# Eight key slots and nine value slots for the sample group, value loads issued by ScalarE, and a projection chunk moved between a sample's picks and its values

## The reference, cut to what matters

```python
q, k, v, u, ga, gp = jnp.split(h @ w_in, SPLITS, axis=-1)     # ga, gp: the gates
...
k_past = k_cache[layer, page_table].reshape(b, -1, N_HEADS, 2, HEAD_DIM)
v_past = v_cache[layer, page_table].reshape(b, -1, N_HEADS, V_DIM)
s_past = jnp.einsum('bqhcd,bkhcd->bhcqk', q, k_past)
s_new = jnp.where(tril, jnp.einsum('bqhcd,bkhcd->bhcqk', q, k_new), NEG)
p = softmax(concat(s_past, s_new) * scale); p = p[:, :, 0] - lam * p[:, :, 1]
return einsum('bhqk,bkhe->bqhe', p[..., :n_past], v_past) + einsum(..., p[..., n_past:], v_new)
```

## Time and profile before

| | |
|---|---|
| Time, median of 3 runs | 2114.14 us (2108.64 to 2119.16) |
| Time of the profiled execution | 2115.86 us |
| Its span, first to last instruction | 2114.1 us |
| Mean granted TensorE clock over the span | 0.988 |
| PE busy, share of the span | 2055.5 us, 97% |
| DVE, ACT, POOL busy | 1117.7, 608.3, 496.7 us |
| Head 7 of phase 1 | from 490 to 564 us |
| Phase 2 | from 564 to 858 us |

### The profile page before, as it was taken

One profiled execution on the slowest core, in us unless ns is written; L12 is line 12 of the kernel. 1 busy time (PEld: TensorE's weight loads), 2 busy tenths in 40 slices (PEclk: granted clock), 3 DMA queues, 4 the chain that ended last, 5 costly groups with the idle time before them and its releaser, 6 DMA issues.

```text
span 2114.1 us, 35690 instructions
## 1 busy us (share of the span) xinstructions
PE 2055.5 (97%) x14393; PEld 1863.8 (88%) x14393; DVE 1117.7 (53%) x1471; ACT 608.3 (29%) x1200; POOL 496.7 (23%) x373
## 2 busy tenths in 40 slices
PE   9999999998887989999999999999999999999999
PEld 8888888886775757999999988999999999999997
DVE  6766666664542333266553443554555555555556
ACT  5444445443311111224112422311221122122120
POOL 5333232421111111242331111311221121122120
PEclk9999999999998989999999999999999999999999
DMA  5222212114388786311224320211110111012112
GB/s 150 57 62 57 61 46 56 37 52 122 120 282 286 252 297 210 97 40 50 87 80 124 118 97 11 70 31 41 50 60 12 61 50 41 31 50 61 31 40 96
DMA packets 190791, 189.18 MB, mean 89 GB/s; under 512 B 21536, under 2 KB 164396, under 8 KB 190516
## 3 DMA queue, kind: packets, MB, share of 16 engines
q1 hardware_dynamic: 175660, 176.53, 26.3%
q10 hardware_dynamic: 14992, 10.62, 1.6%
HBM read 162.73 MB, written 24.62 MB: 89 GB/s over the span
## 4 chain that ended last, share of the span: by engine, by line
PE 93%; DMA 3%; SPq 2%; DVE 1%; issue 1%; POOL 0%; ACT 0%; POOLq 0%; DVEq 0%
PE PS L1488 39%; PE PS L2255 13%; PE PS L1016 6%; PE PS L2010 4%; PE PS L282 4%; PE PS L284 4%; PE PS L283 4%; PE PS L338 3%; PE PS L362 3%; DMA v_pg<-in_cache_v_dram 2%; PE PS L1098 2%; PE PS L351 2%; PE PS L1131 1%; PE PS L1509 1%; PE PS L1521 1%
## 5 line engine op out<-in xcount | busy, mean ns | idle before, releaser
L1475 POOL TENSOR_TENSOR fw_lo<-fw_raw,fw_hi 128x1024 fp32r<-128x1024 f32 x86 | 214.6, 2495 | 823.5 <-ACT fw_hi L1471 823.5
L1488 PE MATMUL PS<-m_hi,fw_hi 128*128 128x384 f32 (+1 forms) x1032 | 228.3, 329 | 0.0
L1488 PE MATMUL PS<-m_lo,fw_hi 128*128 128x384 f32 (+1 forms) x1032 | 227.5, 328 | 0.0
L1488 PE MATMUL PS<-m_hi,fw_lo 128*128 128x384 f32 (+1 forms) x1032 | 227.5, 328 | 0.0
L2383 DVE TENSOR_TENSOR x<-x,PS 128x512 f32<-128x512 f32 x198 | 136.2, 688 | 143.6 <-PE PS L2255 143.3
L1488 PEld LDWEIGHTS PS<-m_hi,fw_lo 128*128 128x128 f32 x1032 | 176.3, 188 | 0.0
L1488 PEld LDWEIGHTS PS<-m_lo,fw_hi 128*128 128x128 f32 x1032 | 176.3, 188 | 0.0
L1488 PEld LDWEIGHTS PS<-m_hi,fw_hi 128*128 128x128 f32 x1032 | 176.0, 188 | 0.4 <-POOL fw_lo L1475 0.2
L282 PE MATMUL PS<-w_hi,act_hi 128*128 128x384 f32 (+1 forms) x456 | 164.7, 361 | 0.0
L284 PE MATMUL PS<-w_hi,act_lo 128*128 128x384 f32 (+1 forms) x456 | 153.6, 337 | 0.0
L283 PE MATMUL PS<-w_lo,act_hi 128*128 128x384 f32 (+1 forms) x456 | 153.1, 336 | 0.0
(11 more groups left out here) (316 smaller groups left out, 4235.0 us busy)
## 6 DMA issues: line engine op xcount, KB each, us to landing
k_ring<-in_cache_k_dram SPq DMA_DIRECT2D x64, 512.0 KB, 5.7
v_pg<-in_cache_v_dram SPq DMA_DIRECT2D x56, 512.0 KB, 6.3
fw_raw<-in_w_up_dram SPq DMA_DIRECT2D x44, 512.0 KB, 3.9
fw_raw<-in_w_in_dram SPq DMA_DIRECT2D x24, 512.0 KB, 4.7
wd_raw<-in_w_down_dram SPq DMA_DIRECT2D x22, 512.0 KB, 4.4
w_raw<-in_w_in_dram SPq DMA_DIRECT2D x21, 512.0 KB, 5.2
out_dram<-raw SPq DMA_DIRECT2D x16, 512.0 KB, 3.7
sa_ring<-ga_scratch SPq DMA_DIRECT2D x8, 544.0 KB, 3.6
```

What stands on the lines that cost most here:

```text
L1475: e.tensor_tensor(fw_lo[slot][:, 0:kts, :], fw_raw[:, 0:kts, :], fw_hi[slot][:, 0:kts, :].bitcast(F32), ALU.subtract).then_inc(fw_tail, 1)
L1488: ins = e.matmul(PS[:, 3 * slot + c, 0:cw], w[slot][:, kt, :], x[:, kt, c0:c0 + cw], start=first and kt == 0, stop=last and kt == KT - 1)
```

## The change

The 17 page slots are divided anew: 8 for keys (one sample's), 9 for values; the last sample's values use the value slots too. With 8 slots the key pages of a sample stand in order, and the scores read them as whole rows of 8 pages. SP loads all 8 keys of the next sample in one go when a sample's scores are done. Value loads past the first nine are issued by ACT, after the copy of the third chunk; so are the weight loads of the gate tiles, in `act_chunk`. The stores of a sample's output move from ACT to SP, one sample later. The third chunk moves between the picks and the values, where page 4 used to follow page 3 with the chunk between them. The samples get 6, 5, 4, 4, 4, 4, 3 and 2 chunks instead of 4 each; the first of sample 0's comes before its scores. In head 7 DVE transposes four key pages, at s = 5 to 8, instead of six at s = 1 to 6. SP issues the first four key pages ahead of the head's k and v stores, and two loads of values later; after the head it waits for the last matmul of the head instead of the stores of its output.

```diff
-                if not proj and 1 <= s <= KEYS_TURNED_EARLY:
-                    dve_turn_keys(e, s - 1)
+                if not proj and s > QT - KEYS_TURNED_EARLY:
+                    dve_turn_keys(e, s - QT + KEYS_TURNED_EARLY - 1)
...
-        KEY_GROUP = NPG // 2
-        RK = 3 * KEY_GROUP
+        HALF = NPG // 2
+        RK = NPG
...
+        mid_pg = [r(f"v_pg{j}", [P, NH * VD]) for j in range(2, 6)]
-        KEYS_TURNED_EARLY = KEYS_EARLY // 2 * 2
+        KEYS_TURNED_EARLY = 4
...
-        late_pg = [r(f"v_pg{j}", [P, NH * VD]) for j in range(2, 5)]
+        late_pg = [r(f"v_pg{j}", [P, NH * VD]) for j in range(6, 9)]
...
-        P_PER = (NC * N_FILL - TT - 1) // NB
+        P_EACH = (6, 5, 4, 4, 4, 4, 3, 2)
...
             e.activation(dst, PS[:, PJ + use % 2, 0:cw], ACT.Copy).then_inc(pj_free, 1)
             if c == NC - 1 and n + 2 <= N_U:
                 fm_head(e, n + 2, n % 2)
+            if c == 0 and n >= 1 and n + 2 <= N_U:
+                fm_load(e, n + 2, gate_cols(n + 2) if n + 2 < N_U else w_in_cols(COL_U))
...
-                                           pages[part, :, :, c:c + QB], start=r == 0 and x == 0, stop=r == 1 and x == XB - 1)
+                                           k_ring[part, :, c:c + QB], start=r == 0 and x == 0, stop=r == 1 and x == XB - 1)
...
         def pe_phase2(e):
             pe_chunk(e, P_FIRST, {})
             for b in range(NB):
                 fill = [lambda p=p: pe_chunk(e, p, {}) for p in chunks_of(b)]
+                if b == 0:
+                    fill[0]()
                 pe_scores_of_sample(e, b)
-                fill[0]()
+                if b:
+                    fill[0]()
                 fill[1]()
                 pe_probs(e, b)
-                for j in range(KEY_GROUP):
+                for f in fill[2:3]:
+                    f()
+                for j in range(NPG + 1):
                     pe_value_page(e, b, j)
-                fill[2]()
-                for j in range(KEY_GROUP, NPG + 1):
-                    pe_value_page(e, b, j)
-                fill[3]()
+                for f in fill[3:]:
+                    f()
...
+        def act_load_values(e, b, first, last):
+            for g in range(RV + b * NPG + first, min(RV + b * NPG + last, NB * NPG)):
+                load_values(e, g)
...
                 act_sample_exp(e, b)
-                act_chunk(e, fill[0])
+                if b:
+                    act_chunk(e, fill[0])
                 act_chunk(e, fill[1])
-                if b:
-                    act_stores(e, b - 1)
-                act_chunk(e, fill[2])
+                for p in fill[2:3]:
+                    act_chunk(e, p)
+                act_load_values(e, b, 0, NPG)
                 act_take_values(e, b)
-                act_chunk(e, fill[3])
+                for p in fill[3:]:
+                    act_chunk(e, p)
...
-            e.wait_ge(k_ld[g % RK // 2], 32 * (g // RK + 1))
+            e.wait_ge(k_ld[g % RK // HALF], HALF * 16 * (g // RK + 1))
...
-            for g in range(2):
-                sp_load_values(e, g)
-            sp_store_kv(e, NH - 1, 1)
             e.wait_ge(b7_free, b_use(NH - 2, True, ("o", TT - 1)) + 1)
             e.wait_ge(kv_st[0], NH // 2 * 64 + 1)
-            for g in range(KEYS_EARLY):
+            for g in range(HALF):
+                sp_load_keys(e, g)
+            sp_store_kv(e, NH - 1, 1)
+            for g in range(HALF, KEYS_EARLY):
                 sp_load_keys(e, g)
...
-            for p in range(TT):
-                sp_chunk(e, p)
-            phase1_over(e)
+            for g in range(2):
+                load_values(e, g)
+            e.wait_ge(b7_full, b_use(NH - 1, False, ("o", TT - 1)) + 1)
+            e.wait_ge(kv_st[1], NH // 2 * 64 + 1)
             sp_load_keys(e, KEYS_EARLY)
             for g in range(2, RV):
-                sp_load_values(e, g)
+                load_values(e, g)
...
             for b in range(NB):
                 e.wait_ge(sc_full, b + 1)
-                for g in range(RK + b * NPG, RK + b * NPG + KEY_GROUP):
-                    if g < NB * NPG:
-                        sp_load_keys(e, g)
...
+                for g in range((b + 1) * NPG, min(b + 2, NB) * NPG):
+                    sp_load_keys(e, g)
                 if b + 2 < NB:
                     e.wait_ge(qb_ready, b + 1)
                     sp_load_queries(e, b + 2)
...
+                if b:
+                    store_outputs(e, b - 1)
```

More of the change, by code:

```diff
@@ L957, in build_step @@
         r = Region(RING, R3)
-        v_pg = [r(f"v_pg{j}", [P, NH * VD]) for j in range(2)] + late_pg
+        v_pg = [r(f"v_pg{j}", [P, NH * VD]) for j in range(2)] + mid_pg + late_pg
         RV = len(v_pg)
@@ L962, in build_step @@
         pg_ld = sem("pg_ld")
-        k_ld = [sem(f"k_ld{j}") for j in range(RK // 2)]
+        k_ld = [sem(f"k_ld{j}") for j in range(RK // HALF)]
         v_ld = [sem(f"v_ld{j}") for j in range(RV)]
@@ L988, in build_step @@
         P_FIRST = TT
-        P_PER = (NC * N_FILL - TT - 1) // NB
-        assert TT + 1 + NB * P_PER == NC * N_FILL
+        P_EACH = (6, 5, 4, 4, 4, 4, 3, 2)
+        assert TT + 1 + sum(P_EACH) == NC * N_FILL and len(P_EACH) == NB
         def chunks_of(b):
-            p = P_FIRST + 1 + b * P_PER
-            return range(p, p + P_PER)
+            p = P_FIRST + 1 + sum(P_EACH[:b])
+            return range(p, p + P_EACH[b])
         ga_dram = nc.dram_tensor("ga_scratch", [P, N_SPILLED, TOK], F32, kind="Internal").ap()
@@ L1051, in pool_chunk @@
                 e.wait_ge(fw_tail, n + 3)
[L1053 to L1056, removed]
         def phase1_over(e):
@@ L1064, in phase1_over @@
                 e.wait_ge(kv_st[i], NH // 2 * 64 + 1)
[L1066 to L1074, removed]
         def queries(g, r, x, part):
@@ L1079, in pe_scores_of_sample @@
         def pe_scores_of_sample(e, b):
-            lo, hi, _ = key_groups(b)
-            pages = k_ring[:, :, :].rearrange("p (g j) n -> p g j n", j=KEY_GROUP)[:, lo:hi + 1:hi - lo, :, :]
             e.wait_ge(qb_ready, b + 1)
@@ L1105, in pe_probs @@
             for j in range(NPG):
-                ins = e.matmul(PS[:, B_PTS, j * NH * NS:(j + 1) * NH * NS], es[:, page_block(b, j) * PAGE:][:, 0:PAGE],
+                ins = e.matmul(PS[:, B_PTS, j * NH * NS:(j + 1) * NH * NS], es[:, j * PAGE:(j + 1) * PAGE],
                                pick_r[b % 2][:, :], start=True, stop=True)
@@ L1122, in pe_value_page @@
                 v = v_new
-            elif b == NB - 1:
-                e.wait_ge(k_ld[(END_SLOT + j) // 2], 32 * (NB * NPG // RK + 1))
-                v = k_ring[:, END_SLOT + j, :]
             else:
@@ L1137, in pe_value_page @@
                 ins.then_inc(os_full, 1)
-        END_SLOT = KEY_GROUP
-        assert (NB * NPG - KEY_GROUP) % RK == 0
         def pe_phase2(e):
@@ L1145, in pe_phase2, with store_output @@
                 fill = [lambda p=p: pe_chunk(e, p, {}) for p in chunks_of(b)]
+                if b == 0:
+                    fill[0]()
                 pe_scores_of_sample(e, b)
-                fill[0]()
+                if b:
+                    fill[0]()
                 fill[1]()
                 pe_probs(e, b)
-                for j in range(KEY_GROUP):
+                for f in fill[2:3]:
+                    f()
+                for j in range(NPG + 1):
                     pe_value_page(e, b, j)
-                fill[2]()
-                for j in range(KEY_GROUP, NPG + 1):
-                    pe_value_page(e, b, j)
-                fill[3]()
-        def act_store(e, b, par, h):
+                for f in fill[3:]:
+                    f()
+        def store_output(e, b, par, h):
             e.dma_start(o_dram[bass.ds(SEQ + b * NS, NS), h * VD:(h + 1) * VD],
@@ L1179, in act_phase2, with store_outputs @@
                 fill = chunks_of(b)
+                if b == 0:
+                    act_chunk(e, fill[0])
                 act_sample_exp(e, b)
-                act_chunk(e, fill[0])
+                if b:
+                    act_chunk(e, fill[0])
                 act_chunk(e, fill[1])
-                if b:
-                    act_stores(e, b - 1)
-                act_chunk(e, fill[2])
+                for p in fill[2:3]:
+                    act_chunk(e, p)
+                act_load_values(e, b, 0, NPG)
                 act_take_values(e, b)
-                act_chunk(e, fill[3])
+                for p in fill[3:]:
+                    act_chunk(e, p)
             act_spill(e, NC * N_FILL - 1)
             fm_head(e, N_U + 1, 1)
-            act_stores(e, NB - 1)
-        def act_stores(e, b):
+            store_outputs(e, NB - 1)
+        def store_outputs(e, b):
             e.wait_ge(os_copied, b + 2)
             for h in range(NH):
-                act_store(e, b, b % 2, h)
+                store_output(e, b, b % 2, h)
         def dve_keys(e, step, b):
@@ L1266, in pool_phase2, with load_page @@
                     pool_chunk(e, p)
```

(31 more changed lines are left out.)

## The result

| | Before | After |
|---|---|---|
| Median of the runs | 2113.79 us (2108.64 to 2119.16, 4 runs) | 2095.37 us (2094.09 to 2096.62, 4 runs) |
| Ratio, 95% interval | | 0.9913, 0.9887 to 0.9938 |
| Profiled execution, span | 2115.86, 2114.1 us | 2095.47, 2093.7 us |

The account below looks back on a forecast made before the run. Some 50 us of PE idle, beside time at 1.2 GHz, were all there was to gain. Phase 2 -44.7, head 7 -9.8, scores +5: -49.5 from 2115.9 gives 2066.4; the median lies 1.7 under: 2065 us, range 2048 to 2091.

Parts of the forecast that it names:

- Scores under DMA load: Scores of samples 1 to 7: value pages landing into them cost PE +5 us, bounds 0 and 27.
- sample 0's 3.9: Extra PE loss per sample when scores run under load, 4.3 us in sample 0's against 0.4 each in samples 1 to 7.
- PE starves at every score: Rival, phase 2 scores: the 3.9 us come in full seven times, 2087 us; chance 0.15.
- ACT's wait in head 7: Chunk 3 of head 7: weight loads moved to ACT wait 6.6 us for POOL's split; PE loses 3, bounds 0 and 6.6.
- the clock's 2.3 us: Head 7: lower-clock time after PE's 10.5 us idle goes too, -2.3 us.
- -10.5, the keys are only turned later: Head 7: DVE's wait for keys goes, as they are turned only from s = 5; PE gains 10.5 us.
- The value wait: Phase 2: PE's 24.8 us wait for value pages goes to nothing with nine value slots.
- its rival: Phase 2: ACT reaches its loads late, half of the 24.8 us and its clock loss remain; near 2085, chance 0.04.
- The copy of the picks: Phase 2: the 0.9 us copy runs beside a 4.36 us chunk; only sample 7 still shows it.
- the 3.2 at which that rival begins: Rival, ScalarE's queue becomes the bound: from 3.2 us a page load the kernel is slower than before; chance 0.03.
- The keys' cover of 3.2 us: Phase 2, four-chunk samples: keys land at 15.7 us after the scores, turned by 20.3, needed at 23.5.
- The lateness forecast by that rival, 6 us: Rival, the keys become the wait: last key lands 6 us later than 15.7; 2088 us, chance 0.13.

Follow-up runs that it names:

- both failed terms away: Changed kernel with value loads past the first nine pages left out and SP issuing head 7's two weight loads: 2061.16 us.
- interleaved: Second half of scores (samples 1 to 7) among next chunk's matmuls: changed kernel, 2095.09 us; also with SP's weights and keys turned by pairs, 2082.14 us.

## Why the prediction was wrong

**The step that failed is "Scores under DMA load", +5 us.** Its size was wrong, not its place. Leaving out the value loads gives 27 us, as much as the upper bound, seven times sample 0's 3.9. That the two agree so closely is in part luck: the rows give 31.8 us of idle and clock, and longer waits for keys and picks take 4.4 back. The reason given for going so low, that half an overlap remains after samples 1 and 2, does not hold: the stands go on to the last sample (2.36 us up to 819.8). And sample 0's case showed one stand, where most samples have two. The likeliest case should have been the rival "PE starves at every score", which was given 0.15 and 2087. It came true.

The prediction was right to suspect that PE's instructions come late: the stands lie 256 instructions apart and end behind a packet of the instruction queue, and most of them go with the value loads. The Trainium skill, Runtime: NRT & Kernel Launch, section Instruction fetch mechanics, has blocks of 16 KiB and says that the cost of crossing from one to the next is mostly hidden. The size agrees with the 16.4 KB of a packet here. The cost is not hidden here: 24.7 us in the kernel after, and 7.4 without most of its value pages. That the packet waits behind page packets inside the DMA engines is argued from these numbers; the trace shows that it starts later under load, not where its request waits.

**The second step is ACT's wait in head 7, taken as 3 us within 0 and 6.6.** It was found where it was put, at chunk 3, for POOL's split. But ACT stood 11.95 us instead of 6.6, for two reasons of like size. The split was over at 525.2, not at 523.0 (533.48 less 10.5), as the query stores in front took SP 8.31 us, 5.10 in the kernel before. And ACT was through with chunk 3 at 513.7, not at 516.4 (526.85 less 10.5). PE lost 6.6 us of idle, and the clock's 2.3 us did not come back: 8.9 us in all, above the bound. Head 7 gained 3 us instead of 9.8. The step "-10.5, the keys are only turned later" had a next wait behind it, which the kernel before with later turning shows.

**What held.** The value wait went to nothing and its rival with it. The value pages run at 4.01 us a sample, forecast 4.32. The copy of the picks is covered in seven samples. ACT issues a page in 0.97 us, far from the 3.2 at which that rival begins. With both failed terms away the kernel takes 2061.2; the sum without them is 2057. The scores' remaining stands, 8.6 us of issue idle in that run, don't explain the 4 us between: the sum has them already, as 2.7 us behind sample 0's scores and a gap of 0.81 us in each sample's 6.44. Keys at 3.6 us instead of 1.2 and the 1.8 us that PE still waits in head 7 come to 4.2; whether it is these, no run tells apart.

**The keys' cover of 3.2 us held only just.** In the sample shown the last half landed 17.6 us after the scores, not at 15.7: the eighth page, issued by 695.0, took some 8.4 us and not 6.6. It was turned at 22.2, not 20.3; over samples 2 to 5 that is 22.2 to 23.1, where PE was to need it at 23.5. Sample 6's keys were turned at 21.9, 2.8 us past the 19.1 of the prediction; its wait stayed at 1.4 us because the stands had stretched the sample. Wherever the stands were cut (4.6 us of waits for keys without values, 7.8 and 18.2 interleaved) the keys became a longer wait. The lateness forecast by that rival, 6 us, was not reached.

In sum: 2065 + 22 (scores) + 5.9 (ACT in head 7) + 4 (the rest) = 2096.9, less 1.7 that the first two don't add: 2095.2, measured 2095.4. This divides the miss but doesn't test it: every added term is worked out from these medians and the forecast, so the sum has to close.

## What to carry to other kernels

A stretch of many small matmuls uses instructions up quickly (here 256 in 2.75 us), and a full DMA can then cost PE time that no wait names: look for idle put down to issue at even distances, and count what a moved transfer will run beside. A single row that shows such a cost was here the likeliest price for every stretch that came under the same condition, not the upper bound. And when a stall is taken away, price the next chain to end there (queries to split to weights, keys to turning) before the gain is booked in full.

## What was not expected of the hardware

In seven of the eight samples exactly 128 matmuls and their weight loads, 256 instructions, lie between two stands of PE; the stands last 0.2 to 3.7 us. All 15 end 2.2 to 3.0 us after a 16.4 KB packet of the instruction queue starts, whether the DMA engines are full by then or all but idle; under the page loads that packet comes later. With all of the scores spread between wider matmuls the issue idle fell from 28.1 to 8.4 us (8.2, and 0.2 in the chunk) at the same DMA share (0.73 in phase 2), while waits for keys grew from 0.7 to 7.0. Eight stores of the queries took SP's queue 8.31 us, 5.10 us in the kernel before.
